# A hybrid transformer pair on one core: other distances between the input tiles, the feed-forward units and the weights in SBUF, modulo 256 bytes

## The chip, the cores and the metric

One core of one Trainium2 chip. The metric is the device time of one execution in microseconds; of the kernel before there are three such times and one profiled execution.

## The reference

Two transformer blocks in float32 on one sequence of 256 tokens and 1024 features. Block one: modulation from a condition vector, a mixer (state-space scan beside forgetting attention), layer norm, a feed-forward pair of 1024 x 4096 and back with squared relu, layer norm. Block two has two layers; each is

```python
x = x + 0.5 * swiglu_ffn(rms_norm_2(x, ffn1_norm[i]), ffn1_w_in[i], ffn1_w_out[i])
h = rms_norm_2(x, mix_norm[i])
# y: pool_mixer (layer 0) or nsa_mixer (layer 1) of h
x = x + y
x = x + memory_cross_attention(rms_norm_2(x, xattn_norm[i]), rms_norm_2(mem, mem_norm[i]),
                               xattn_w_q[i], xattn_w_kv[i], xattn_w_o[i])
x = x + 0.5 * swiglu_ffn(rms_norm_2(x, ffn2_norm[i]), ffn2_w_in[i], ffn2_w_out[i])
```

`swiglu_ffn` is `(silu(h @ w_g) * (h @ w_u)) @ w_out` with 2816 units. Nearly all arithmetic is the products with weight matrices, some 265 MB of float32 weights that are each read once.

## The kernel before

Activations stand transposed in SBUF: feature tile k of 128 features is `x[:, k, :]`, 256 tokens wide, 1024 bytes a partition. Every product with a weight matrix is made exact enough by splitting both operands in a high and a low part (float32r) and adding three matmuls: `mm3` (lines 448 to 451) issues high x high (449), high x low (450), low x high (451) for one 128 x 128 block of weights and 256 columns. In the profile the line names the pair: L449 is `x_hi` with `w_hi`, L450 `x_lo` with `w_hi`, L451 `x_hi` with `w_lo`.

Weights come in slots of 2048 columns (8192 bytes a partition), four slots in a ring (`RING`, `SLOT`). SP loads slot n into `raw[n % 4]`; ACT rounds it into `w_hi` (L1058); DVE writes the rest into `w_lo` (L1600), which takes the place of `raw`; TensorE multiplies. The order of slots is the list `STAGES`.

Two helpers hold nearly all calls of `mm3`. `gemm_a` has the weights stationary and the activations moving: a weight load of 128 columns, then a matmul of 256. `gemm_b` has the activations stationary (128 tokens) and 256 columns of weights moving. The attentions' `share` and the `filling` during a norm do the same in pieces. A feed-forward pair is `ffn_in` (activations from the input tiles `x_hi`, `x_lo`; 22 slots of 16 calls of `mm3`) and `ffn_out` (from the units `hid_hi`, `hid_lo`; 16 slots of 11 calls); in the first block both have 16 slots of 16 calls. Memory tiles `mh`, `ml` (`m1h`, `m1l` later) feed the keys and values of the cross attentions; they too are used in both roles. `compression` (line 943) is a short stage of the sparse attention: row k of `bk_hi[b]` or `bk_lo[b]`, 60 columns or 240 bytes long, is stationary, for k = 0 to 15 one behind the other, and a row of `w_hi` or `w_lo` of 256 columns moves.

Tensors are allocated one behind the other, each start rounded up to 32 bytes, by `sb(name, shape)`; the first of them, `raw` and `w_lo`, start at byte 16,512 of a partition, `w_hi` follows 32,768 bytes later, then `X`, a pad `ahead_of_x`, `x_hi`, `x_lo`, a pad `behind_x`, then `memN`, parameters, small tiles, a work space and, last, the `arena` of 80 KB. The units, memory tiles, attention tiles and `bk` are places in the arena at multiples of 1024 bytes; only its start decides their address modulo 256. Modulo 256 the weights (and raw, X) start at 128; `x_hi` and `x_lo` at 64; `memN` at 160; the arena and all that is placed in it at 64.

Of the kernel before, what the change touches and what calls it, by code (L numbers as in the profile page):

```python
# [25 lines left out]
P = 128  # L26
# [111 lines left out]
def build(nc, w, xT_d, memT_d, par_d, rows_d, cond_d, out_d):  # L138
# [5 lines left out]
    with ctx:  # L144
        def sb(name, shape, dt=F32, stack=ctx):
            return stack.enter_context(nc.sbuf_tensor(name, shape, dt))
# [7 lines left out]
        w_lo = [sb(f"w_lo{b}", [P, SLOT], F32R) for b in range(RING)]  # L154
        w_hi = [sb(f"w_hi{b}", [P, SLOT], F32R) for b in range(RING)]
        X = sb("X", [P, KC, S])
        sb("ahead_of_x", [P, 240])
        x_hi = sb("x_hi", [P, KC, S], F32R)
        x_lo = sb("x_lo", [P, KC, S], F32R)
        sb("behind_x", [P, 152])  # L160
        memN = sb("memN", [P, KC, S])
        par = sb("par", [P, NPAR])
        rows = sb("rows", [P, 64])
# [2346 lines left out]
```

## Time and profile before

| | us |
|---|---|
| three runs | 1609.32, 1624.85, 1606.76 (median 1609.32) |
| the profiled execution, its own time | 1607.69 |
| its span, first to last instruction | 1606.0 |
| TensorE matmuls busy | 1553.4 (97%) |
| TensorE weight loads busy | 1522.9 (95%) |
| VectorE / ScalarE / GpSimd busy | 1067.6 / 835.3 / 171.3 |

All terms below are made against the profiled execution. A busy share counts overlapping matmuls as one stretch; it says that TensorE is never idle for long, not how fast it works.

### The profile page before, as it was taken

The page shows a single profiled execution, that of the slowest core. Times are in us where ns is not written, and L with a number is a line of the kernel's source. Part 1 is how long each engine was busy: PE and PEld are TensorE (multiplying, and loading weights), DVE is VectorE, ACT ScalarE, POOL GpSimd, SP SyncE. Part 2 cuts the span into 40 slices and gives each one's busy share as a digit, 9 for nine tenths or more (in the row PEclk, how much of TensorE's full clock was granted, in tenths as well). Part 3 has the DMA queues.
Part 4 walks back from the last instruction along what each step waited for, and adds up shares of the span by engine and source line. Part 5 has one row for each costly group of instructions (what it writes and reads, how often), then busy time and mean ns, then how long its engine had stood idle before and what let it go on. Part 6 is the DMA issues. An engine that isn't in the chain of part 4 may idle for free.

```text
span 1606.0 us, 31707 instructions
## 1 busy us (share of the span) xinstructions
PE 1553.4 (97%) x12998; PEld 1522.9 (95%) x12998; DVE 1067.6 (66%) x1557; ACT 835.3 (52%) x1209; POOL 171.3 (11%) x223
## 2 busy tenths in 40 slices
PE   6999999999999999999999999999999999999998
PEld 6999999999999999999999999999998889999998
DVE  6787887886556666565666656665655677566654
ACT  6466656755545444464544455444565555354442
POOL 2013300400012600020100010000100111010000
PEclk9899999999999999999999999999999999999999
DMA  9552873465553654562455565545654014255553
GB/s 372 230 211 105 341 289 117 161 247 189 185 183 106 218 198 163 196 228 102 177 194 185 173 217 186 200 162 195 223 187 152 28 54 167 100 182 200 183 175 122
DMA packets 45125, 293.14 MB, mean 183 GB/s; under 512 B 5200, under 2 KB 6496, under 8 KB 15712
## 3 DMA queue, kind: packets, MB, share of 16 engines
q1 hardware_dynamic: 41184, 265.49, 47.3%
q0 software_dynamic: 3840, 26.23, 4.2%
q8 instruction: 72, 1.18, 0.3%
q14 instruction: 29, 0.24, 0.0%
HBM read 288.02 MB, written 3.67 MB: 182 GB/s over the span
## 4 chain that ended last, share of the span: by engine, by line
PE 78%; DVE 11%; ACT 5%; DMA 4%; issue 1%; SPq 0%; DVEq 0%; POOL 0%; POOLq 0%
PE G L449 23%; PE G L450 23%; PE G L451 23%; DVE w_lo L1600 4%; PE O L640 3%; ACT w_hi L1058 2%; DMA mod_w<-w_ada 1%; PE L L1019 1%; PE T L626 1%; DMA mod_x<-w_ada 1%; PE L L888 1%; DVE X L1726 1%; DVE XB L1870 1%; DMA raw<-w_xk 1%; ACT x_hi L1135 1%
## 5 line engine op out<-in xcount | busy, mean ns | idle before, releaser
L1600 DVE TENSOR_TENSOR w_lo<-raw,w_hi 128x2048 fp32r<-128x2048 f32 (+1 forms) x256 | 541.1, 2117 | 262.7 <-ACT w_hi L1058 262.0
L449 PE MATMUL G<-x_hi,w_hi 128*128 128x256 f32 x2176 | 610.3, 280 | 10.4 <-DVE w_lo L1600 7.0
L450 PE MATMUL G<-x_lo,w_hi 128*128 128x256 f32 x2176 | 606.0, 279 | 0.0
L451 PE MATMUL G<-x_hi,w_lo 128*128 128x256 f32 x2176 | 606.0, 279 | 0.0
L1058 ACT ACTIVATE w_hi<-raw 128x2048 fp32r<-128x2048 f32 (+1 forms) x260 | 458.8, 1768 | 151.2 <-DMA raw<-w_ffout 37.8
L449 PEld LDWEIGHTS G<-x_hi,w_hi 128*128 128x128 f32 x2176 | 411.7, 189 | 14.4 <-DVE w_lo L1600 9.2
L451 PEld LDWEIGHTS G<-x_hi,w_lo 128*128 128x128 f32 x2176 | 412.6, 190 | 0.0
L450 PEld LDWEIGHTS G<-x_lo,w_hi 128*128 128x128 f32 x2176 | 411.6, 189 | 0.1
L449 PE MATMUL G<-hid_hi,w_hi 128*128 128x256 f32 x1280 | 359.0, 280 | 2.9 <-DVE hid_lo L1632 2.3
L451 PE MATMUL G<-hid_hi,w_lo 128*128 128x256 f32 x1280 | 355.1, 277 | 0.0
L450 PE MATMUL G<-hid_lo,w_hi 128*128 128x256 f32 x1280 | 355.0, 277 | 0.0
L449 PEld LDWEIGHTS G<-hid_hi,w_hi 128*128 128x128 f32 x1280 | 240.8, 188 | 4.3 <-issue 1.8
L451 PEld LDWEIGHTS G<-hid_hi,w_lo 128*128 128x128 f32 x1280 | 241.2, 188 | 0.0
L450 PEld LDWEIGHTS G<-hid_lo,w_hi 128*128 128x128 f32 x1280 | 240.5, 188 | 0.1
L1164 ACT ACTIVATE hid_hi<-hb 128x256 f32 (+3 forms) x104 | 46.9, 451 | 250.6 <-DVE hb L1763 250.6
L1751 DVE TENSOR_TENSOR gu<-G,R 128x512 f32<-128x512 f32 x88 | 60.8, 690 | 73.1 <-PE G L451 72.7
L1127 ACT ACTIVATE Pr<-Lm,nmax 128x128 f32<-128x128 f32 (+1 forms) x112 | 51.6, 461 | 78.9 <-DVE nmax L1663 78.6
L1135 ACT ACTIVATE x_hi<-X,par 128x256 fp32r<-128x256 f32 x56 | 28.3, 505 | 97.5 <-DVE X L1726 97.4
L449 PE MATMUL G<-w_hi,x_hi 128*128 128x256 f32 (+2 forms) x256 | 75.9, 296 | 0.2 <-ACT vs L1478 0.2
L2313 POOL TENSOR_TENSOR acc<-acc,T 128x256 f32<-128x256 f32 x62 | 48.0, 774 | 238.0 <-ACT T L1137 235.6
L451 PE MATMUL G<-w_hi,x_lo 128*128 128x256 f32 (+2 forms) x256 | 72.1, 281 | 0.0
L450 PE MATMUL G<-w_lo,x_hi 128*128 128x256 f32 (+2 forms) x256 | 72.0, 281 | 0.0
(411 smaller groups left out, 1826.4 us busy)
## 6 DMA issues: line engine op xcount, KB each, us to landing
raw<-w_f1in SPq DMA_DIRECT2D x44, 1024.0 KB, 4.8
raw<-w_f2in SPq DMA_DIRECT2D x44, 1024.0 KB, 4.8
raw<-w_f1out SPq DMA_DIRECT2D x32, 704.0 KB, 4.1
raw<-w_f2out SPq DMA_DIRECT2D x32, 704.0 KB, 4.1
raw<-w_ffin SPq DMA_DIRECT2D x16, 1024.0 KB, 4.8
raw<-w_ffout SPq DMA_DIRECT2D x16, 1024.0 KB, 4.8
mod_x<-w_ada POOLq DMA_DIRECT2D x12, 1024.0 KB, 7.7
mod_w<-w_ada POOLq DMA_DIRECT2D x8, 1024.0 KB, 13.4
```

The costliest lines, as they stand in the source:

```text
L449: mm(out, l_hi, r_hi, start=start, stop=False)
L450: mm(out, l_hi, r_lo, start=False, stop=False)
L451: return mm(out, l_lo, r_hi, start=False, stop=stop)
L626: last = nc.tensor.transpose(T[u % 2][0:w_, c * P:(c + 1) * P], Pr[u % 2][:, c * P:c * P + w_], ident[:])
L640: last = mm(O[t][:, (h % per) * hd:(h % per + 1) * hd], PT[u % 2][0:w_, c, :], pv(h, c), start=c == 0, stop=c == nch - 1)
L1058: act_(w_hi[n % RING][:, 0:s.size], raw[n % RING][:, 0:s.size], ACT.Copy).then_inc(s_hi, 1)
L1127: act_(Pr[u % 2][:, 0:nk], Lm[u % 2][:, 0:nk], ACT.Exp, bias=nmax[:, col:col + 1], scale=-1.0, accum_out=ssum[:, col:col + 1]).then_inc(q( ...
L1135: act_(x_hi[:, ft, :], X[:, ft, :], ACT.Copy, scale=pc(*gain(ft))).then_inc(q(name + ".hi"), 1)
L1164: act_(hid_hi[:, bass.ds(c0, chunks), :], hb[slot % 2][:, 0:width].rearrange("p (k c) -> p k c", k=chunks), ACT.Copy).then_inc(q(s.name + ...
L1600: v.tensor_tensor(w_lo[b][:, 0:s.size], raw[b][:, 0:s.size], w_hi[b][:, 0:s.size].bitcast(F32), ALU.subtract).then_inc(s_lo, 1)
L1751: v.tensor_tensor(gu[slot % 2][:], tiles2(G[j % 2]), bc(R[:].unsqueeze(1), [P, 2, S]), ALU.mult)\
L2313: ins = g_.tensor_tensor(acc[:], acc[:], src[:, ft, :], ALU.add)
```

## The change

The two pads get other sizes. `ahead_of_x` shrinks from 960 to 128 bytes, `behind_x` from 608 to 192.

```diff
         X = sb("X", [P, KC, S])
-        sb("ahead_of_x", [P, 240])
+        sb("ahead_of_x", [P, 32])
         x_hi = sb("x_hi", [P, KC, S], F32R)
         x_lo = sb("x_lo", [P, KC, S], F32R)
-        sb("behind_x", [P, 152])
+        sb("behind_x", [P, 48])
         memN = sb("memN", [P, KC, S])
```

Weights, `raw` and `X` stay where they are. `x_hi` and `x_lo` move down by 832 bytes, from 64 to 0 modulo 256. Everything behind them moves down by 1248 bytes: the arena and its tiles from 64 to 96 modulo 256, `memN` from 160 to 192. Nothing else differs: the instructions, their order, their waits and the DMAs are the same.

## Rows read from the trace of the kernel before

**Rows 1.** The page: span, share of the span, tenths in 40 slices

```profile
span 1606.0 us, 31707 instructions
...
PE 1553.4 (97%) x12998; PEld 1522.9 (95%) x12998; DVE 1067.6 (66%) x1557; ACT 835.3 (52%) x1209; POOL 171.3 (11%) x223
...
PE   6999999999999999999999999999999999999998
...
PEclk9899999999999999999999999999999999999999
```

**Rows 2.** The page's chain that ended last; the waits: who waited, us, times, longest

```profile
PE 78%; DVE 11%; ACT 5%; DMA 4%; issue 1%; SPq 0%; DVEq 0%; POOL 0%; POOLq 0%
PE G L449 23%; PE G L450 23%; PE G L451 23%; DVE w_lo L1600 4%; PE O L640 3%; ACT w_hi L1058 2%; DMA mod_w<-w_ada 1%; PE L L1019 1%; PE T L626 1%; DMA mod_x<-w_ada 1%; PE L L888 1%; DVE X L1726 1%; DVE XB L1870 1%; DMA raw<-w_xk 1%; ACT x_hi L1135 1%
...
PE G L449 <- DVE w_lo L1600: 11.0, 11, 1.9
```

**Rows 3.** The page's groups: count, busy us, mean ns of one, idle before

```profile
L450 PE MATMUL G<-x_lo,w_hi 128*128 128x256 f32 x2176 | 606.0, 279 | 0.0
...
L450 PE MATMUL G<-hid_lo,w_hi 128*128 128x256 f32 x1280 | 355.0, 277 | 0.0
```

**Rows 4.** Matmuls by stretch: from:to, length, busy us (count), clock, DMA share, GB/s

```profile
77.00:103.00 26.00, 26.00 (x223) 1.00 0.69 249
181.00:199.00 18.00, 17.92 (x153) 1.00 0.94 353
...
335.00:482.00 147.00, 147.00 (x1248) 1.00 0.57 201
556.00:640.00 84.00, 84.00 (x744) 1.00 0.54 183
641.00:697.00 56.00, 56.00 (x495) 1.00 0.63 207
789.00:901.00 112.00, 112.00 (x991) 1.00 0.53 185
902.00:963.00 61.00, 61.00 (x541) 1.00 0.63 210
...
1428.00:1540.00 112.00, 112.00 (x990) 1.00 0.53 185
```

**Rows 5.** Groups of matmuls of 400 to 420 us, units and input tiles

```profile
L450 PE MATMUL G<-hid_lo,w_hi 128*128 128x256 f32 x33 | 9.3, 281 | 0.0
...
L450 PE MATMUL G<-x_lo,w_hi 128*128 128x256 f32 x25 | 7.0, 281 | 0.0
```

**Rows 6.** As rows 4: two token-stationary slots, and one with 48 moving columns

```profile
127.40:132.80 5.40, 5.40 (x48) 1.00 0.59 194
134.90:140.30 5.40, 5.40 (x48) 1.00 0.43 176
...
1196.00:1200.00 4.00, 4.00 (x38) 0.99 0.73 258
```

**Rows 7.** Timeline of `compression`: start us, duration; line 449 at k = 4, 5, 8 to 15

```profile
1186.12 0.28 PE L449 MATMUL G<-w_hi,bk_hi 128*60 128x256 f32 x1
...
1186.47 0.28 PE L449 MATMUL G<-w_hi,bk_hi 128*60 128x256 f32 x1
...
1187.53 0.28 PE L449 MATMUL G<-w_hi,bk_hi 128*60 128x256 f32 x1
...
1187.88 0.28 PE L449 MATMUL G<-w_hi,bk_hi 128*60 128x256 f32 x1
...
1188.23 0.28 PE L449 MATMUL G<-w_hi,bk_hi 128*60 128x256 f32 x1
...
1188.59 0.28 PE L449 MATMUL G<-w_hi,bk_hi 128*60 128x256 f32 x1
...
1188.93 0.28 PE L449 MATMUL G<-w_hi,bk_hi 128*60 128x256 f32 x1
...
1189.27 0.28 PE L449 MATMUL G<-w_hi,bk_hi 128*60 128x256 f32 x1
...
1189.61 0.28 PE L449 MATMUL G<-w_hi,bk_hi 128*60 128x256 f32 x1
...
1189.97 0.28 PE L449 MATMUL G<-w_hi,bk_hi 128*60 128x256 f32 x1
```

## The prediction

> **What bounds the kernel now.** I read the head of the page first. TensorE matmuls are busy 97% of the span and its weight loads 95%; the tenths stand at 9 in nearly every slice, and the granted clock too, which is its upper level of 2.4 GHz [rows 1]. The chain that ended last is 78% TensorE, and 69% of the span lies on lines 449 to 451, the three matmuls of `mm3`; the largest wait of the matmuls for a split weight tile in the running stream is 11.0 us in eleven pieces [rows 2]. So what counts is how often a matmul of `mm3` starts, not what it waits for. The groups of the page cannot tell that, since matmuls overlap (each record is 277 to 279 ns long, [rows 3]); a count over a stretch can. Two or three matmuls already run when a stretch begins, so the pace is the length divided by (count less 2).
>
> The windows show two paces and nothing between [rows 4]. From 335 to 482 us, 147.00 us hold 1248 matmuls: 117.98 ns each, or 117.8 without a short wait; 77 to 103 us gives the same (26.00/221 = 117.6). From 556 to 640, 641 to 697, 789 to 901, 902 to 963 and 1428 to 1540 us it is 84.00/742 = 113.2, 56.00/493 = 113.6, 112.00/989 = 113.2, 61.00/539 = 113.2 and 112.00/988 = 113.4 ns. I call them the long step, 117.8, and the short step, 113.3; the difference is 4.4 ns. It isn't the clock (1.00 in both), and it isn't the operation: input tiles and feed-forward units both run at the long step between 400 and 420 us, with records of 281 ns, and both at the short one later [rows 4, 5]. Nor is it traffic: the DMA share is 0.57 in the long stretch and 0.53 to 0.63 in the short ones. A stretch keeps its step over 1,000 matmuls and more. So at today's distances a stream with weights stationary falls into one of two patterns. Where the token tile is stationary and the weights stream past (`gemm_b`), I find only the long step: 5.40/46 = 117.4 ns in both windows shown [rows 6].
>
> **What the change does to addresses.** Let d be the start of the stationary tile less that of the moving one, modulo 256. All slots, rows and halves of the large tiles are multiples of 512 bytes, so d is one number per pairing. Before, the pads of 960 and 608 bytes put input tiles and arena 64 bytes below the weights: d = +64 in `gemm_a` for input tiles and units, -64 in `gemm_b`. After, with 128 and 192 bytes, d = 128 for the input tiles in both roles; for units +32, for memory tiles +32 and -32. X and the weights stay. Everything from memN to the arena's end moves by the same -1248 bytes, so the pairings inside it (attention, transposes, PV) keep their d: no cost. No instruction, wait or DMA is added or removed. DVE and ACT work is not on the path (DVE 66%, ACT 52% busy, [rows 1]); were they slowed by it, TensorE would cover it until a split tile comes late, which today is those 11 us. I take nothing for them.
>
> **The price.** The program has 3,920 calls of `mm3`, 11,760 matmuls. The four second-block feed-forward pairs are 4 x 22 x 48 = 4,224 with input tiles and 4 x 16 x 33 = 2,112 with units; rows show them short. The first block's pair is 2 x 16 x 48 = 1,536, long but for its tail. Token-stationary slots (about 16 of 48, 768) and the windows at 77 and 181 us (221 and 151) are long too. That places 6,336 short and 2,676 long; the other 2,748, in pieces between waits, I halve. Short: 7,700 (4,900 with input tiles, 2,800 with units). Long: 4,050.
> - All short steps become long: 7,700 x 4.44 = +34 us.
> - Those of the input tiles alone: 4,900 x 4.44 = +22 us; of the units alone: +12 us.
> - All long steps become short: 4,050 x 4.44 = -18 us.
> - Below the short step: where the moving operand has only 48 columns the stream goes at the pace of weight loads, 4.00/36 = 111 ns [rows 6]. All matmuls at that: a further 11,760 x 2.3 = -27 us, -45 in all. That is the lower bound.
> - Upper bound: the longest triple of the sweep below takes 0.36 us, 120 ns for one. All at that: 7,700 x 6.7 + 4,050 x 2.2 = +60 us.
>
> **What the trace says of other distances.** One stage sweeps d by itself. In `compression` the stationary tile is row k of `bk`, 240 bytes each, so d = -64 - 16k, from k = 0 to 15, with the weights moving; a load has 60 columns there, not 128. Rows of line 449 give the length of a triple: three matmuls with k = 4 (d = 128) take 1186.47 - 1186.12 = 0.35 us, 117 ns each; with k = 8 (d = +64) 0.35; with k = 10 (d = +32) 0.36; with k = 14 (d = -32) 0.36; but with k = 12 and k = 13 (d = 0 and -16) 0.34 us, 113 ns each, and k = 11, whose last matmul overlaps the load of row 12, 0.34 too [rows 7]. A reading is good to 0.01 us, 3 ns for one matmul. So the step does hang on d in units of 16 bytes, the short one occurs in a narrow band (d = 0 and -16), and at the new distances 128, +32 and -32 this stage shows the long step. The proxy is weak at one place: at d = +64 (k = 8) it has the long step too, where `gemm_a` with 128 columns runs short two times in three. A load with more columns may have its band elsewhere, around +64 for all I can see. Between reading 'bands are narrow, and +64 lies in one' and 'the band of 128-column loads is unknown', I take the first, since one band of two or three values in sixteen is all that the sweep shows, and -64 has none.
>
> The rows show that the step depends on where two SBUF reads lie to each other [rows 7]. The Trainium skill ("TensorE: Matmul & The Clock Gate", Part 2, step 1) says that the weight load and the moving operand have independent read ports, so that one takes no bandwidth from the other; "SBUF — State Buffer" (Who interferes with whom) adds that PE waits for no other engine. By that rule addresses change nothing and the sum is 0; the sweep speaks against it, yet a pattern that each start draws afresh could look like a sweep, so it is a rival.
>
> **The forecast.** Both pairings lose the short step: 1607.7 + 34 = 1642 us against the profiled execution; I say 1641. The median of the three runs, 1609.3, is 1.6 above that execution, which leaves it within the same range. Its own range is 1630 to 1648. Chance 0.30.
>
> **Rivals.**
> 1. All short (other side). For 128-column loads, 128 and +32 lie inside the band, and the streams that drew the long pattern now can't; `gemm_b`, too, since 128 is the same distance in both roles. For it: the sweep's 60-column load covers less than one turn of 256 bytes, a 128-column load two, so the sweep may not carry over; against it: 117 and 120 ns at 128 and at +32 [rows 7]. 1607.7 - 18 = 1590 us. It decides as soon as the input tiles of the four large pairs stay short and the first block's pair turns short. Chance 0.28; with the load-bound pace below it (1607.7 - 45 = 1563 us) 0.06 more.
> 2. Input tiles lose, units keep: 1607.7 + 22 = 1630 us. For it: the input tiles move by a quarter turn, the units only by 32 bytes from +64. Chance 0.12.
> 3. Nothing that lasts: the step is drawn at each start of a stream and not set by d, or gains of one pairing meet losses of the other (units alone 1620, input tiles half kept 1600). One of the three runs of before, at 1624.9, is 17 us above another, as if one or more long streams had drawn the other pattern. 1608 us, from 1598 to 1620. Chance 0.20.
> 4. A third, longer step, as in the sweep's 120 ns: up to 1607.7 + 60 = 1668 us. Chance 0.04.
>
> **How the numbers follow.** About 1% is what a measurement can tell from no change: 16 us, below 1593 or above 1625. Faster: most of rival 1's 0.28 lies just past the edge, I count 0.22 of it, plus 0.06: 0.28. Slower: 0.30 + 0.10 + 0.04 = 0.44. Within 1%: 0.28. The range 1588 to 1646 leaves out the load-bound pace, the third step and a little at both edges, together under 2 in 10; it is wide because both signs hold real chances.
>
> **What would show it.** In the profile after, the windows over the four large pairs: at 117.8 ns a window of 112.00 us holds about 953 matmuls, at 113.3 ns 990, at 111 ns 1,011. The records' mean length tells the same (276 or 281 ns). If the input stage is long and the unit stage short, it is rival 2. Token-stationary slots: 48 matmuls in 5.40 us if long, 50 if short. In `compression` nothing changes, as weights and `bk` shift by 32: the short triples should move from k = 12 and 13 to k = 14 and 15, where d is now 0 and -16; if they stay, d modulo 256 isn't what counts. Wrong it would be, above all, if the four large pairs keep the short step at d = 128 and +32.

## The result and the profile after

The changed kernel is slower: 1646.51 us, median of four runs (1644.39 to 1648.45), against 1608.04 us for the kernel before (1603.88 to 1624.85). The ratio is 1.0241, with a 95% interval of 1.0209 to 1.0274. The profiled execution took 1645.3 us, its span is 1643.5 us against 1606.0 before: 37.5 us more. Against the forecast: 1641 was said, on the right side and for the reason given, but the time lies 0.5 us above the top of the range.

The head of the page after, in the same columns as [rows 1] and [rows 2]:

```profile
span 1643.5 us, 31707 instructions
...
PE 1594.5 (97%) x12998; PEld 1564.9 (95%) x12998; DVE 1063.4 (65%) x1557; ACT 840.1 (51%) x1209; POOL 171.2 (10%) x223
...
PEclk9899999999999999999999999999999999999999
...
PE G L449 24%; PE G L451 23%; PE G L450 23%; DVE w_lo L1600 4%; PE O L640 3%; ACT w_hi L1058 2%; DMA mod_w<-w_ada 2%; DMA mod_x<-w_ada 1%; PE L L1019 1%; PE T L626 1%; PE L L888 1%; DMA raw<-w_xk 1%; DVE X L1726 1%; DVE XB L1870 1%; ACT x_hi L1135 1%
```

The shape has not changed: the same 12,998 matmuls, busy 97% of a longer span, the same clock, the same lines on the chain. Busy time of the matmuls grew by 41.1 us; that of VectorE fell by 4.2 us, that of ScalarE rose by 4.8. The page's groups put the growth into the records of `mm3`. The row of the waits behind them answers to the last of [rows 2], 9.1 us after and 11.0 before, so it isn't this wait; none of the matmuls' waits grew by more than 0.6 us:

```profile
L450 PE MATMUL G<-x_lo,w_hi 128*128 128x256 f32 x2176 | 615.8, 283 | 0.0
...
L450 PE MATMUL G<-hid_lo,w_hi 128*128 128x256 f32 x1280 | 360.1, 281 | 0.0
```

```profile
PE G L449 <- DVE w_lo L1600: 9.1, 11, 1.8
```

A matmul with input tiles is 283 ns long and one with units 281, where [rows 3] have 279 and 277. The pace is in the windows of matmuls (from:to, length, busy us and count, granted clock, DMA share, GB/s), which answer to [rows 4]:

```profile
341.00:488.00 147.00, 147.00 (x1241) 1.00 0.55 199
563.00:647.00 84.00, 84.00 (x710) 1.00 0.50 176
653.00:709.00 56.00, 56.00 (x476) 1.00 0.59 199
804.00:916.00 112.00, 112.00 (x946) 1.00 0.50 178
922.00:983.00 61.00, 61.00 (x518) 1.00 0.60 204
987.00:1099.00 112.00, 112.00 (x946) 1.00 0.50 181
1459.00:1571.00 112.00, 112.00 (x946) 1.00 0.50 178
```

With input tiles 112.00/944 = 118.6 ns from one matmul to the next, in all three large windows, where [rows 4] had 990 or 991 matmuls (113.3 ns). With units 61.00/516 = 118.2 ns, where there were 541 (113.2). Even the stretch that was long before is a little longer: 147.00/1239 = 118.6 against 118.0. No window of these two kinds holds the short step any more. The new step isn't an even one either: in the trace the single steps between 805 and 915 us are 114 to 123 ns long, where those of before between 790 and 900 us are all 113 or 114.

A window's count is good to one matmul, 0.1 ns in the windows of 112 us and 0.2 in those of 61. Below I also use means of the time from the start of one record of `mm3` to the start of the next, over all pairs less than 130 ns apart, which leaves the waits out. After, they are 118.72 ns for input tiles and 118.32 ns for units in `gemm_a`, means that held 114.53 and 114.52 ns before. What such steps take above 113.33 ns adds up over the kernel as follows.

| | before, us | after, us | difference |
|---|---|---|---|
| input tiles in `gemm_a` | 7.7 | 34.6 | +26.9 |
| units | 4.5 | 18.9 | +14.4 |
| all other calls of `mm3` | 4.4 | 5.6 | +1.1 |
| gaps of 130 ns and more behind a matmul of `mm3`, less 113.33 each | 54.3 | 48.6 | -5.6 |
| sum | 70.9 | 107.8 | +36.9 |

Each entry, the differences too, is rounded by itself. 36.9 of the 37.5 us of the span are in these rows. What is left is 0.5 us before the first matmul (12.8 against 12.4 us) and 0.3 behind matmuls of other lines (183.5 against 183.2), to rounding.

### The profile page after: what moved, and what is told of

Same layout as the page of the kernel before. It is cut to its first block, busy times and chain, and to the rows that moved or that the text cites. A ratio compares the mean times of both kernels' runs of the same rounds, so it can differ in the third digit from the quotient of the medians.

```text
span 1643.5 us, 31707 instructions
## 1 busy us (share of the span) xinstructions
PE 1594.5 (97%) x12998; PEld 1564.9 (95%) x12998; DVE 1063.4 (65%) x1557; ACT 840.1 (51%) x1209; POOL 171.2 (10%) x223
## 4 chain that ended last, share of the span: by engine, by line
PE 79%; DVE 9%; DMA 5%; ACT 4%; issue 1%; POOL 1%; SPq 0%; DVEq 0%; POOLq 0%
PE G L449 24%; PE G L451 23%; PE G L450 23%; DVE w_lo L1600 4%; PE O L640 3%; ACT w_hi L1058 2%; DMA mod_w<-w_ada 2%; DMA mod_x<-w_ada 1%; PE L L1019 1%; PE T L626 1%; PE L L888 1%; DMA raw<-w_xk 1%; DVE X L1726 1%; DVE XB L1870 1%; ACT x_hi L1135 1%
## 5 line engine op out<-in xcount | busy, mean ns | idle before, releaser
L449 PE MATMUL G<-x_hi,w_hi 128*128 128x256 f32 x2176 | 619.6, 285 | 7.0 <-DVE w_lo L1600 5.5
L451 PE MATMUL G<-x_hi,w_lo 128*128 128x256 f32 x2176 | 615.8, 283 | 0.0
L450 PE MATMUL G<-x_lo,w_hi 128*128 128x256 f32 x2176 | 615.8, 283 | 0.0
L449 PE MATMUL G<-hid_hi,w_hi 128*128 128x256 f32 x1280 | 364.1, 284 | 2.2 <-DVE hid_lo L1632 2.2
L450 PE MATMUL G<-hid_lo,w_hi 128*128 128x256 f32 x1280 | 360.1, 281 | 0.0
L451 PE MATMUL G<-hid_hi,w_lo 128*128 128x256 f32 x1280 | 360.1, 281 | 0.0
```

The source lines that it names most:

```text
L449: mm(out, l_hi, r_hi, start=start, stop=False)
L450: mm(out, l_hi, r_lo, start=False, stop=False)
L451: return mm(out, l_lo, r_hi, start=False, stop=stop)
```

## The experiments

Every kernel of this section is the kernel before with other pads, and in three of them with input tiles that start inside their allocation; nothing else. d is the start of the stationary tile less that of the moving one, modulo 256, as in the prediction; where two numbers stand, the first is that of the input tiles with the weights stationary, the second that of the units. Before it is +64 and +64, after 128 and +32. The runs of one group share the runs of the kernel before.

### One half of the change at a time

Only the units and memory tiles move (+64, +32):

```diff
-        sb("behind_x", [P, 152])
+        sb("behind_x", [P, 96])
```

> Input tiles back at their old address (d = +64 to the weights, modulo 256), units and memory tiles where the change put them (+32). Theory A (each pairing has its own distance, and both new ones lie outside the band of the short step): the input stages of the four large feed-forward pairs run at 113.3 ns a matmul again, the unit stages at 118.35 ns as after the change; the excess of the unit matmuls after over before is about 14 us, so 1608 + 14 = 1622 us. Theory B (one cause common to all, such as the place of the arena): everything stays long, 1646 us. Theory C (the step is drawn at the start of a stream, distances don't matter): stages of either kind at either step, no pattern.

Only the input tiles move (128, +64):

```diff
-        sb("ahead_of_x", [P, 240])
+        sb("ahead_of_x", [P, 32])
...
-        sb("behind_x", [P, 152])
+        sb("behind_x", [P, 360])
```

> The other half alone: input tiles where the change put them (d = 128), the arena with units and memory tiles exactly at its old address (+64). Theory A: input stages at 118.65 ns, unit stages at 113.3 ns in the four large pairs; the excess of the input-tile matmuls after over before is about 26 us, so 1608 + 26 = 1634 us; the two halves together make the 38 us of the change. Theory B: 1608 or 1646 us, nothing between. Theory C: no pattern.

Measured, against 1611.68 us for the kernel before (19 runs, 1601.29 to 1620.27): units alone 1628.31 us, ratio 1.0123 (1.0068 to 1.0177); input tiles alone 1632.66 us, 1.0140 (1.0085 to 1.0195). The two add to 2.6%, beside 2.4% for the whole change. The windows of units alone; the first, third and fourth have input tiles, the second and the last units:

```profile
799.00:911.00 112.00, 112.00 (x989) 1.00 0.54 185
912.00:973.00 61.00, 61.00 (x518) 1.00 0.59 202
977.00:1089.00 112.00, 112.00 (x954) 1.00 0.52 181
1447.00:1559.00 112.00, 112.00 (x989) 1.00 0.52 185
1561.00:1617.00 56.00, 56.00 (x475) 1.00 0.45 153
```

The windows of input tiles alone; the first and third have input tiles, the others units:

```profile
795.00:907.00 112.00, 112.00 (x946) 1.00 0.51 178
913.00:974.00 61.00, 61.00 (x520) 1.00 0.60 206
978.00:1090.00 112.00, 112.00 (x946) 1.00 0.51 181
1101.00:1162.00 61.00, 61.00 (x539) 1.00 0.63 212
```

The tile that moved lost the short step everywhere: 518 and 946 matmuls, just as after. The tile that stayed at +64 had both steps, side by side in one kernel: input tiles 989 (113.5 ns) and 954 (117.6), units 539 (113.6) and 520 (117.8). So each pairing pays for its own distance. And at +64 a stream takes one of two steps and keeps it: the three input windows of the first kernel are the same code with the same distances, and each held its step for 112 us. I call this a draw, since no trace shows what decides it. In that kernel about half of the matmuls with input tiles drew the long step where [rows 4] have a quarter of them, which costs 14.6 - 7.7 = 6.9 us in its profiled execution and goes beside the 18.9 - 4.5 = 14.4 us, 0.9%, of its units.

The input tiles alone show one thing more. At 128, too, a stream takes one of two steps, 118.7 ns as above or 120.0: the stage with input tiles from 555 us on held the longer one, 84.00/701 = 119.8.

```profile
556.00:640.00 84.00, 84.00 (x703) 1.00 0.50 175
```

### Other addresses with the same distances

All of the input tiles and the arena move by an odd multiple of 256 bytes (+64, +64):

```diff
-        sb("ahead_of_x", [P, 240])
+        sb("ahead_of_x", [P, 48])
...
-        sb("behind_x", [P, 152])
+        sb("behind_x", [P, 24])
```

> Input tiles and arena at the distances of the kernel before modulo 256 (-64 below the weights, both), but with pads of 192 and 96 bytes, so that they lie 768 and 1280 bytes lower than before. If only the distance modulo 256 counts: 113.3 ns in the four large pairs, 1608 us. If a larger period counts (512 or 1024 bytes), the steps differ: 1620 us or more.

Every tensor, weights too, moves by 128 bytes (+64, +64):

```diff
+        sb("ahead_of_all", [P, 32])
         with ExitStack() as a:
             raw = [sb(f"raw{b}", [P, SLOT]) for b in range(RING)]
```

> The kernel before with everything, weights included, moved up by 128 bytes: all distances as before, all addresses modulo 256 others (weights 0, input tiles and arena 192). Theory A (distances): as before, 1608 us, 113.3 ns in the large pairs. Rival (the tile's own place modulo 128 or 256 counts, such as an input tile that starts at 0 modulo 256): another step, 1620 us or more.

Measured, ten runs each: 1612.7 us, ratio 0.9997 (0.9969 to 1.0025), and 1611.4 us, 1.0006 (0.9976 to 1.0037). So neither a distance modulo 512 or 1024 nor a shift of everything by 128 bytes counts, to 0.4%; with the distances modulo 256 unchanged, the time is unchanged. Windows of the first kernel, both with input tiles:

```profile
787.00:899.00 112.00, 112.00 (x953) 1.00 0.50 178
...
974.00:1086.00 112.00, 111.85 (x987) 1.00 0.53 186
```

The input stage at 787 us drew the long step, 112.00/951 = 117.8 ns, where the kernel before had the short one in its profile [rows 4]. What its input tiles take above 113.33 ns is 8.0 us all the same, beside 7.7 before, since other stages drew short; its units take 9.2 us beside 4.5. One window of 991 matmuls is worth 991 x 4.44 = 4.4 us, so a few such draws would be enough for the 19 us between the runs of the kernel before. That they make them isn't shown, since there is one trace of each kernel.

The second kernel puts a harder question to the distance, in its sweep inside `compression`. Moved by 128 bytes, row k has the place modulo 256 that row k + 8 or k - 8 had. If a row's own place set the step, the short triples of k = 12 and 13 [rows 7] would now stand at k = 4 and 5; if the distance sets it, they stay. They stay, in both passes. Line 449 is 450 in this kernel; the first two rows are k = 4 and 5, the others 12 to 15:

```profile
1187.47 0.28 PE L450 MATMUL G<-w_hi,bk_hi 128*60 128x256 f32 x1
1187.82 0.28 PE L450 MATMUL G<-w_hi,bk_hi 128*60 128x256 f32 x1
...
1190.28 0.28 PE L450 MATMUL G<-w_hi,bk_hi 128*60 128x256 f32 x1
1190.62 0.28 PE L450 MATMUL G<-w_hi,bk_hi 128*60 128x256 f32 x1
1190.96 0.28 PE L450 MATMUL G<-w_hi,bk_hi 128*60 128x256 f32 x1
1191.31 0.28 PE L450 MATMUL G<-w_hi,bk_hi 128*60 128x256 f32 x1
```

1187.82 - 1187.47 = 0.35, but 1190.62 - 1190.28 = 0.34 and 1190.96 - 1190.62 = 0.34. One limit remains for the long streams, and what was expected of this kernel passes over it: a shift by 128 leaves every address modulo 128 as it was. The weights start at 0 modulo 128 in every kernel here, so d = +64 and -64 are also just the cases in which the other tile starts at 64 modulo 128. That place alone doesn't set the step (0 and 128 share one, and so do +32 and -96, with different steps in the table below), but for the short step no run separates the distance from that place.

### A map of distances

Five kernels put input tiles and units at other multiples of 32 bytes, three (with a view that starts 16 or 8 bytes into a tile) the input tiles at distances near +64. The pads, ahead and behind, in floats of 4 bytes: 16 and 40; 56 and 48; 40 and 48; 0 and 64; 8 and 40. The view, with pads of 240 and 24:

```diff
-        x_hi = sb("x_hi", [P, KC, S], F32R)
+        x_hi = sb("x_hi", [P, KC * S + 64], F32R)[:, 4:4 + KC * S].rearrange("p (k s) -> p k s", k=KC)
```

and the same for `x_lo`; the second has pads of 232 and 32, the third 240 and 24 with 2 in place of 4.

> Input tiles 64 bytes above the weights modulo 256 (d = 192, that is -64, where weights are stationary), units and memory tiles at 128. The pieces so far gave: short step possible at +64 and, for token-stationary slots, at -64; never at 128 (input tiles) or +32 (units). If d and its mirror image behave alike and it doesn't matter which tile it is, the input stages run short for some streams at -64 and the unit stages never at 128: about 1608 + 14 = 1622 us. If 128 is bad for input tiles alone, 1608 us.

> Input tiles 32 bytes below the weights (d = +32), units 64 above (d = -64). By distance alone: input stages never short (118.3 ns, as the units had at +32), unit stages short for some streams: 1608 + 24 = 1632 us. If +32 is bad only for tiles in the arena: 1608 us.

> Input tiles 96 bytes below the weights (d = +96), units at the same place modulo 256 (d = 0). Narrow band around +64 and -64: both long, 1640 to 1650 us. A band of 64 to 127: input tiles short, 1620 us. The sweep inside the kernel before had its short triples at d = 0 and -16: if that carries over to loads of 128 columns, the units are short at 0.

> The two swapped: input tiles at d = 0, units at +96. By distance alone the steps of the run before this one change places: each distance gives the same mean step for input tiles as for units within 0.2 ns. Time then 1608 plus 26 us times the input tiles' excess and 14 us times the units' excess, as shares of the long step's.

> Input tiles 32 bytes above the weights (d = -32), units 96 above (d = -96). If a distance and its mirror image behave alike, input stages run at 118.3 ns as at +32 and unit stages at 117.3 to 118.8 ns as at +96, never short, about 1645 us. If the sign counts, other steps, or a short one.

> Input tiles 48 bytes below the weights (d = +48), units as in the kernel before (+64). The tile starts 16 bytes into an allocation, nothing else differs. If the short step needs 64 to the byte or its 16-byte line: input stages long throughout, 1608 + 24 = 1632 us. If there is a band around 64: short for some or all streams, at best all, then the time falls below the kernel before, to 1600 us.

> The same on the other side: input tiles 80 bytes below the weights (d = +80), units at +64. Narrow: 1632 us. Band: 1600 to 1612 us.

> Input tiles 56 bytes below the weights (d = +56), half a line of 16 bytes off, units at +64. If lines of 16 bytes count, the step is that of +64 or of +48; if bytes count, one between. A step of its own would say that the unit isn't 16 bytes.

Measured, with the kernel before at 1613.41 us for the first four and 1612.35 for the rest. The steps are means of start to start as above, counted up to 150 ns here, since at some of these distances single ones pass 130. Where a distance has more than one step, the mean mixes its streams.

| d of input tiles / units | us | ratio (95%) | step, input tiles | step, units |
|---|---|---|---|---|
| -64 / 128 | 1633.17 | 1.0125 (1.0060 to 1.0190) | 116.3, either 113.3 or 117.8 | 118.7, in one stream 120.0 |
| +32 / -64 | 1637.97 | 1.0155 (1.0090 to 1.0219) | 118.3 | 117.1, either 113.3 or 117.8 |
| +96 / 0 | 1645.15 | 1.0199 (1.0137 to 1.0261) | 117.7, either 117.3 or 118.7 | 119.9 |
| 0 / +96 | 1648.46 | 1.0220 (1.0163 to 1.0277) | 119.9 | 117.8, either 117.3 or 118.7 |
| -32 / -96 | 1640.72 | 1.0171 (1.0097 to 1.0244) | 117.0, either 116.7 or 117.8 | 119.9 |
| +48 / +64 | 1629.87 | 1.0123 (1.0052 to 1.0194) | 118.6, either 116.7 or 119.1 | 113.8 |
| +80 / +64 | 1635.66 | 1.0135 (1.0078 to 1.0191) | 119.2 | 115.7 |
| +56 / +64 | 1638.51 | 1.0155 (1.0099 to 1.0211) | 120.1 | 114.9 |

Windows that carry the table, all of matmuls. Distance -64 (input tiles, first kernel of the table), where one kernel has both steps, 988 and 953 matmuls:

```profile
799.00:911.00 112.00, 112.00 (x988) 1.00 0.52 185
...
977.00:1089.00 112.00, 112.00 (x953) 1.00 0.52 181
```

Distance 0 for units (third kernel), 61.00/510 = 119.6 ns; and for input tiles (fourth kernel), 112.00/934 = 119.9:

```profile
923.00:984.00 61.00, 61.00 (x512) 1.00 0.60 200
```

```profile
803.00:915.00 112.00, 112.00 (x936) 1.00 0.50 178
```

Distance -32 for input tiles and -96 for units (fifth kernel), 116.7 and 119.8 ns:

```profile
801.00:913.00 112.00, 112.00 (x962) 1.00 0.51 179
917.00:978.00 61.00, 61.00 (x511) 1.00 0.58 197
```

Distance +48 (sixth kernel), two input windows of one kernel, 119.1 and 116.7 ns:

```profile
793.00:905.00 112.00, 112.00 (x942) 1.00 0.50 179
...
1441.00:1553.00 112.00, 112.00 (x962) 1.00 0.52 179
```

Distance +80 (seventh kernel) and +56 (eighth), input tiles, 112.00/939 = 119.3 and 112.00/934 = 119.9 ns:

```profile
796.00:908.00 112.00, 112.00 (x941) 1.00 0.50 178
```

```profile
801.00:913.00 112.00, 112.00 (x936) 1.00 0.51 179
```

Two things follow. First, the short step exists only at +64 and -64 among the eleven distances run, and 16 bytes to either side of +64, even 8 bytes below it (+56: 119.9 ns in each of the three large stages with input tiles), it is gone. Second, ±64 aren't the only distances with more than one step, drawn for a stream (+48 above, also +96, -32 and 128), but at the others none of the steps is short. The mirror of the kernel before, input tiles at -64, gives the same two steps. No kernel was faster than the one before, and none of these distances offers more than it has.

### The sweep inside `compression`, read again

No kernel was run for this; all of them contain the sweep. It is where the prediction took its band from. Durations of a triple (three matmuls from the start of line 449 with row k to its start with the next row, in ns from the starts of the records), by d:

```
d                        +64  +48  +32  +16    0  -16  -32
before, both passes      352  350  353  347  340  342  353
d 128 for units, pass 1  352  350  352  348  340  342  353
  the same, pass 2       345  357  354  350  350  349  359
-64 for units, pass 1    350  350  354  351  353  357  352
  the same, pass 2       357  356  351  347  340  342  353
after, pass 1            345  357  355  349  351  350  349
  the same, pass 2       349  351  354  351  354  360  351
```

The second and third lines are the experiment with input tiles at -64 and units at 128. Its arena starts 64 bytes lower than before, modulo 256, so the short triples should move from k = 12 and 13 to k = 8 and 9, and in the first pass they do. The start us, duration and tiles of line 449 with k = 8 to 11, in that pass:

```profile
1206.75 0.28 PE L449 MATMUL G<-w_hi,bk_hi 128*60 128x256 f32 x1
...
1207.09 0.28 PE L449 MATMUL G<-w_hi,bk_hi 128*60 128x256 f32 x1
...
1207.43 0.28 PE L449 MATMUL G<-w_hi,bk_hi 128*60 128x256 f32 x1
...
1207.79 0.28 PE L449 MATMUL G<-w_hi,bk_hi 128*60 128x256 f32 x1
```

1207.09 - 1206.75 = 0.34, 1207.43 - 1207.09 = 0.34, then 0.36. After, at k = 14 and 15, where d is 0 and -16, there is no such pair (k = 13 to 15 of the first pass; the last row is the first matmul of what follows):

```profile
1219.36 0.28 PE L449 MATMUL G<-w_hi,bk_hi 128*60 128x256 f32 x1
...
1219.71 0.28 PE L449 MATMUL G<-w_hi,bk_hi 128*60 128x256 f32 x1
...
1220.06 0.28 PE L449 MATMUL G<-w_hi,bk_hi 128*60 128x256 f32 x1
...
1220.41 0.28 PE L449 MATMUL G<-x_hi,w_hi 128*128 128x256 f32 x1
```

The table shows more than one order of durations. There are a few patterns, each a list of durations by d that returns in other kernels to within 1 to 3 ns but for the first rows of a pass; a pass runs in one of them. One has 340 and 342 ns at 0 and -16, one has 345 at +64 and 357 at +48, one has 353 and 357 to 360 at 0 and -16. A fourth, in the kernel with input tiles at 0, has its short triples at +96 and +80 (343 and 341 ns). The kernel before had the first in both passes of its profile, the changed kernel the two others. So the sweep fits the long streams: the step goes with the distance modulo 256 and with a pattern that is drawn.

## Why the prediction was wrong at its edge and right in its direction

**What bounds the kernel.** Right. The wait for split weight tiles didn't grow (9.1 against 11.0 us), VectorE and ScalarE stayed covered, and 41.4 of the 42.5 us that the steps added are in the `gemm_a` calls with input tiles and units.

**The count of short steps.** Right: 7,700 said, 4,900 with input tiles and 2,800 with units; in the trace of before 7,706 steps of `mm3` were shorter than 115.5 ns (matmuls within streams, without waits), 4,700 with input tiles and 2,806 with units, the rest elsewhere.

**Both pairings lose the short step.** Right, and separately for each (units alone 1.2%, input tiles alone 1.4%). Rival 1, all short, would have shown 990 matmuls in 112 us, and the windows have 946. Rival 2, units keep, would have left them at 541, and they have 518.

**The size of the step that takes its place.** This is the term that failed. The prediction took 117.8 ns, the long step of the distances in use, for the step at the new ones, and wrote 953 matmuls for a window of 112 us; it is 946. At 128 the step is 118.7 ns, in a short stream of after 120.0, and at +32 it is 118.3. So the short ones cost 4,900 x 5.3 + 2,800 x 5.0 = 40 us and not 34, and steps that were long already, priced at nothing, cost about 0.9 and 0.5 ns each: 1,710 and 985 of them in `gemm_a`, 2 us. With 1.1 for the other calls, 5.6 us less in gaps and 0.8 outside `mm3`, 42 becomes 38, beside the 37.5 measured. The case for this stood in the text as rival 4 with 0.04: a third, longer step. What was missed is that it need not come everywhere or at 120 ns; one of 118.5 is enough to pass the top of the range. The sweep couldn't have given the size: its 0.36 us at +32, read as 120 ns a matmul, is 353 ns in the table above, or 117.7, and its 0.35 at 128 is 352 ns [rows 7]. The prediction read from it that the new distances are "long" and had no row for how long, with loads of 128 columns. The likeliest case's own range, 1630 to 1648, holds the time; the range over all cases was cut at 1646, inside of it, and that cut left no room for the term. That the sum came as near as it did is in part luck: steps that cost 8 us more than priced (42 against 34) met gaps that were 5.6 us shorter, which nobody had forecast.

**The proxy.** Its conclusion held, its reading didn't. The prediction took the sweep for one band of short distances. Other passes have no short pair at 0 and -16, and in none has the triple at +64 the 340 ns of three short steps. The step at one d can't be read from one pass, and the test that was named, that the short triples move to k = 14 and 15 or else d isn't what counts, was a false test: after, neither happened, and d does count.

**Rival 3, the step is drawn.** True of the distances in use and a mistake as a forecast. Streams do draw their step at ±64, which would explain the spread of the kernel before (the two runs that the prediction compares are 18 us apart, not 17). But after, all draws are from a list without the short one: its four runs lie within 4.1 us.

**Token-stationary.** `gemm_b` with input tiles, d from -64 to 128, went from a mean of 116.9 ns to 117.9, long as before; all calls outside the two large groups take 1.1 us more together, which the sum had at nothing. That `gemm_b` has "only the long step" at -64 was a reading of one trace, though. The stage that held 180 matmuls in 21.00 us from 205 us on in the kernel before (118.0 ns) held 179 in 20.00 us from 207 us on in the one with everything moved by 128 (113.0), at the same d.

**The rule that was weighed.** The windows of after and of the two halves (946 against 990 matmuls) decide it by measurement: where the tiles lie changes the pace. The sweep of the kernel with everything moved, whose short triples stayed with the distance, says that it is where the two lie to each other, so that weight load and moving operand aren't independent here. Whether they meet at a port, no run shows. The sentence of the Trainium skill ("TensorE: Matmul & The Clock Gate", Part 2, step 1) that the two have independent read ports would make the ratio 1.000; it is 1.0241.

**Open.** What in the chip makes the step depend on the distance, and what draws the pattern of a stream, isn't shown; no run set the draw. For the long streams distance isn't told from the other tile's own place modulo 128; a run that moves all tensors by 32 bytes would tell. Nor is it shown why 60-column loads have other short distances than 128-column loads. That ±64 are the only short distances holds for the eleven that were run, out of more that are possible.

## What to carry to other kernels

Where a stream of float32r matmuls with 256 columns, a weight load before each, is what bounds a kernel, allocate the stationary and the moving tiles with their starts 64 bytes apart modulo 256, as here, where the weights also start at a multiple of 128, and guard that distance: a pad elsewhere that shifts one of them costs up to 120.0/113.3, or 6%, of the stream's time. The busy share doesn't show it (97% before and after) and the mean record hardly (279 against 283 ns); a count of matmuls over a window does. Before such a kernel is compared with another, look at which step its long streams drew, since one draw is worth up to 4.4 us here. A range around a value that was read at other conditions should reach to the largest value that the trace shows at all (here 360 ns for a triple, 120.0 for one, at k = 2 in the first pass of the sweep).

## What was not expected of the hardware

- The step from one matmul to the next, in an unbroken stream at 2.4 GHz, is 113.3, 116.7, 117.3, 117.8, 118.3, 118.7, 119.1, 119.2 or 120.0 ns in the mean, according to the distance modulo 256 of two SBUF starts and to a pattern; [rows 4] show two of these.
- Eight bytes matter: at +56 the large stages with input tiles run at 119.9 ns, at +64 at 113.3 or 117.8.
- A stream of 991 matmuls keeps the pattern that it has from its start to its end, and the same streams of one kernel, code and distances equal, differ.
- Distance 0, the two tiles aligned to each other, is the worst with -96 and +56: 120.0 ns in every long stream.
